# A hybrid recurrent and sparse-attention block on one core: index scores by pairs of heads, recurrence levels over all four quarters of TensorE's array

## What is computed

```python
h = rms_norm(x, norm_mix_pre); z = h @ w_in
# head group 1: RWKV-7, 8 heads of 64, one state (64 x 64) per head, step by step in time
state = state * w_t + (state @ -kk_t) (kk_t * a_t)^T + v_t k_t^T ;  o_t = state @ r_t
# head group 2: sparse attention; an index of 8 heads of 64 chooses the 256 keys of each query
act = relu(einsum('bqhd,bsd->bqsh', qi, ki) * idx_scale)
score = einsum('bqsh,bqh->bqs', act, wi)         # then top-k per query, softmax over those keys
x += rms_norm(concat(y_rwkv, y_attention) @ w_out); x += rms_norm(sqrelu(...) @ w2); x += ...gate...
```

## Time and profile before

| | us |
|---|---|
| median of 3 runs (2139.25 to 2147.84) | 2145.26 |
| profiled execution, and its span | 2152.6, 2150.9 |
| PE busy, PEld busy, DVE busy, ACT busy | 1841.4, 1496.7, 1058.0, 605.5 |
| index scores, first product to last addition | 330.65 to 409.13 |
| recurrence, steps with levels (s = 0 to 7) | 791.5 to 1000 |
| mean granted TensorE clock (share of full speed) | 0.901 |

### The profile page before, as it was taken

The page is one execution under the profiler, slowest core; times in us unless marked ns, Lnnn a source line. Parts: engine busy times, 40 slices in busy tenths (PEclk is TensorE's granted clock), DMA queues, the critical chain, the costliest instruction groups (busy, mean ns, idle before and its releaser), DMA issues. The chain is left out here.

```text
span 2150.9 us, 34217 instructions
## 1 busy us (share of the span) xinstructions
PE 1841.4 (86%) x13992; PEld 1496.7 (70%) x13992; DVE 1058.0 (49%) x1927; ACT 605.5 (28%) x963; POOL 516.4 (24%) x375
## 2 busy tenths in 40 slices
PE   1999968799489969998597699999999999966993
PEld 0876754388367769997486588888888888855782
DVE  6166724599855635775314644253442533536203
ACT  4245413477355533332221200000000000013220
POOL 3133300032022201222243322222222222204233
PEclk9999985699789989998796699999999999985996
DMA  2135440123111050210510011111111111100201
GB/s 99 56 111 174 132 129 27 39 69 115 51 42 40 11 194 28 76 33 15 201 40 20 30 49 48 44 46 46 49 49 49 49 49 49 49 20 0 88 11 78
DMA packets 75000, 134.75 MB, mean 63 GB/s; under 512 B 5824, under 2 KB 49888, under 8 KB 74368
## 3 DMA queue, kind: packets, MB, share of 16 engines
q1 hardware_dynamic: 45760, 118.38, 16.7%
q10 hardware_dynamic: 29120, 14.68, 2.4%
HBM read 96.86 MB, written 36.18 MB: 62 GB/s over the span
## 5 line engine op out<-in xcount | busy, mean ns | idle before, releaser
L440 POOL TENSOR_TENSOR w_ffn_lo<-w_ffn_raw,w_ffn_hi 128x1024 fp32r<-128x1024 f32 x64 | 153.7, 2403 | 547.7 <-ACT w_ffn_hi L436 532.9
L436 ACT ACTIVATE w_ffn_hi<-w_ffn_raw 128x1024 fp32r<-128x1024 f32 x62 | 65.8, 1062 | 614.7 <-PE ffn_acc L463 320.1
L461 PE MATMUL ffn_acc<-h_hi,w_ffn_hi 128*128 128x512 f32 x512 | 200.3, 391 | 10.6 <-DVEq L565 10.6
L462 PE MATMUL ffn_acc<-h_lo,w_ffn_hi 128*128 128x512 f32 x512 | 200.1, 391 | 0.0
L463 PE MATMUL ffn_acc<-h_hi,w_ffn_lo 128*128 128x512 f32 x512 | 200.0, 391 | 0.0
L448 PE MATMUL ffn_acc<-ffn_hi,w_ffn_hi 128*128 128x512 f32 x512 | 199.2, 389 | 0.0
L449 PE MATMUL ffn_acc<-ffn_lo,w_ffn_hi 128*128 128x512 f32 x512 | 199.2, 389 | 0.0
L450 PE MATMUL ffn_acc<-ffn_hi,w_ffn_lo 128*128 128x512 f32 x512 | 199.2, 389 | 0.0
L581 DVE TENSOR_TENSOR y<-y,ffn_acc 128x2048 f32<-128x2048 f32 x32 | 73.2, 2288 | 240.5 <-PE ffn_acc L450 240.5
L461 PE MATMUL z_acc<-h_hi,w_in_first_hi 128*128 128x512 f32 x304 | 122.3, 402 | 14.4 <-ACTq L502 10.4
L573 DVE TENSOR_SCALAR ffn_relu<-ffn_acc 128x1024 f32<-128x1024 f32 x32 | 39.2, 1225 | 169.3 <-PE ffn_acc L463 169.3
(11 more groups left out here) (327 smaller groups left out, 4095.0 us busy)
## 6 DMA issues: line engine op xcount, KB each, us to landing
w_ffn_raw<-w_ffn SPq DMA_DIRECT2D x64, 512.0 KB, 3.5
rwkv_factors<-factors_then_masks ACTq DMA_DIRECT2D x28, 512.0 KB, 6.3
factors<-rwkv_factors SPq DMA_DIRECT2D x32, 448.0 KB, 6.9
w_in_first_raw<-w_in SPq DMA_DIRECT2D x19, 512.0 KB, 4.0
w_in_raw<-w_in SPq DMA_DIRECT2D x12, 512.0 KB, 4.2
x_in<-xT SPq DMA_DIRECT2D x8, 512.0 KB, 6.6
zT<-z_out SPq DMA_DIRECT2D x8, 512.0 KB, 2.9
w_out_raw<-w_out SPq DMA_DIRECT2D x8, 512.0 KB, 4.0
```

The lines of the kernel that those rows point to most:

```text
L436: act.activation(self.hi[u][:, :], self.raw[:, u, :], ACT.Copy).then_inc(self.rounded, 1)
L440: pool.tensor_tensor(self.lo[u][:, :], self.raw[:, u, :], self.hi[u][:, :].bitcast(F32), ALU.subtract).then_inc(self.split, 1)
L461: pe.matmul(acc[:, cut], w.hi[u][:, col], hi[:, k, cut], start=(k == 0), stop=False)
L462: pe.matmul(acc[:, cut], w.hi[u][:, col], lo[:, k, cut], start=False, stop=False)
```

## The change

Index scores: PE takes two heads at a time, one on each half of the array's rows, chunk of keys by chunk of keys, into its own PSUM tensor each; there are two such pairs of tensors and four relu buffers. PE waits for both relus of the pair before the last. The mask is loaded after the first queries.

Recurrence: T and T transposed now lie with chunks in opposite partition halves. The factor A is written with its two chunks exchanged (one DVE instruction becomes two). `levels` does in every slot the `take_x` of one half of the heads together with the `take_sum` of the other, head by head; per head there are then products over all four quarters. It waits for the ACT copy and the DVE merges of both before its first product. `multiply_b` computes one more product per head (8 more per call), since T and its transpose need the product of A and B in both layouts. In `own_chunk` the K·A products go to the opposite column half and another PSUM bank than the K·R products; so ACT waits for `tg_done` before its first copy of piece 4. `copy_x` and `add_level` are now one per slot.

```diff
-                dve.scalar_tensor_tensor(out[:, A_T, :], kk[:, :], -1.0, e_before[:, :], ALU.mult, ALU.mult)
+                for c in range(2):
+                    by_chunk = lambda x: x.rearrange("p (i c t) -> p i c t", i=TILES, c=2)
+                    dve.scalar_tensor_tensor(by_chunk(out[:, A_T, :])[:, :, 1 - c, :], by_chunk(kk[:, :])[:, :, c, :], -1.0, by_chunk(e_before[:, :])[:, :, c, :], ALU.mult, ALU.mult)
...
+    over = ((half[0], half[1]), (half[1], half[0]))
...
-        ps_x = [ctx.pb(f"ps_level_x{h}", [P, HALF], F32) for h in range(2)]
-        ps_t = [ctx.pb(f"ps_level_sum{h}", [P, 2, HH, N], F32) for h in range(2)]
+        ps_l = [ctx.pb(f"ps_level{h}", [P, 4, HH, N], F32) for h in range(2)]
...
+            def levels(hx, hs, sx, ss, lx, ls):
+                x, m = 0 <= sx < TILES, 0 <= ss < TILES
+                if x and lx == 0:
+                    pe.wait_ge(cut1[hx], sx + 1)
+                    pe.wait_ge(t0_ready[hx], sx + 1)
+                elif x:
+                    pe.wait_ge(level_added[hx], LV * sx + lx)
+                if m:
+                    pe.wait_ge(level_x_copied[hs], LV * ss + ls + 1)
+                    need(pe, level_added[hs], LV * ss + ls)
                 for hd in range(HH):
+                    if x:
+                        for a, b in over:
+                            last_x = pe.matmul(ps_l[hx][b, 0, hd, :], mx[hx][sx % 3][a, hd, BA, :], tt[hx][sx % 3][a, 0, hd, :], start=True, stop=True)
+                    if m:
+                        for a, b in over:
+                            last_s = pe.matmul(ps_l[hs][b, 2, hd, :], xs[hs][b, hd, :], tt[hs][ss % 3][b, 1, hd, :], start=True, stop=True)
+                        if ls < LV - 1:
+                            for a, b in over:
+                                last_s = pe.matmul(ps_l[hs][a, 1, hd, :], tt[hs][ss % 3][b, 1, hd, :], xs[hs][b, hd, :], start=True, stop=True)
...
-                    for c in half:
+                    for c, o in over:
                         for e, k in enumerate(half):
-                            pe.matmul(bank[h][c, e, q * 4 * N:(q * 4 + 1) * N], F[k, 2 * h + q, A_T, c], F[k, 2 * h + q, B_T, c], start=True, stop=True)
+                            pe.matmul(bank[h][c, e, q * 4 * N:(q * 4 + 1) * N], F[k, 2 * h + q, A_T, o], F[k, 2 * h + q, B_T, c], start=True, stop=True)
+                            pe.matmul(bank[h][o, e, (q * 4 + 3) * N:(q * 4 + 4) * N], F[k, 2 * h + q, B_T, c], F[k, 2 * h + q, A_T, o], start=True, stop=True)
...
-                    for x, which in enumerate((KA, KR)):
-                        for hd in range(HH):
-                            for c in half:
-                                last = pe.matmul(bank[h][c, 0, (2 * hd + x) * N:(2 * hd + x + 1) * N], mx[h][f % 3][c, hd, which, :],
-                                                 tm[h][f % 3][c, TV, hd % 2, hd // 2, :], start=True, stop=True)
+                    for hd in range(HH):
+                        v = tm[h][f % 3][:, TV, hd % 2, hd // 2, :]
+                        for a, b in over:
+                            pe.matmul(bank[h][b, 0, hd * N:(hd + 1) * N], mx[h][f % 3][a, hd, KA, :], v[a], start=True, stop=True)
+                        for c in half:
+                            last = pe.matmul(bank[h][c, 1, hd * N:(hd + 1) * N], mx[h][f % 3][c, hd, KR, :], v[c], start=True, stop=True)
...
-                for h in range(2):
-                    if n % 2 == 0:
-                        take_x(h, s, n // 2)
-                    else:
-                        take_sum(h, s, n // 2)
+                if n % 2 == 0:
+                    levels(0, 1, s, s if n else s - 1, n // 2, n // 2 - 1 if n else LV - 1)
+                else:
+                    levels(1, 0, s, s, n // 2, n // 2)
...
+                        if 0 <= t < TILES:
+                            act.wait_ge(tg_done[h], t + 1)
                         if f < TILES:
                             act.wait_ge(own_products[h], f + 1)
...
-        rl = ctx.sb("index_relu", [P, 2, SEQ], F32)
-        ps = ctx.pb("ps_index", [P, 2, SEQ], F32)
+        rl = ctx.sb("index_relu", [P, 4, SEQ], F32)
+        ps = [[ctx.pb(f"ps_index{v}{e}", [P, SEQ], F32) for e in range(2)] for v in range(2)]
...
+            for m, (j, t, b) in enumerate(units):
                 keys = (t + 1) * P
                 pe.wait_ge(loaded[j % 2], 16 * (j // 2 + 1))
+                if m >= 2:
+                    pe.wait_ge(relued, 2 * (m - 1))
+                for c in range(0, keys, HALF):
+                    cut = slice(c, min(c + HALF, keys))
+                    for e in range(2):
+                        f = slice(e * IDX, (e + 1) * IDX)
+                        last = pe.matmul(ps[m % 2][e][:, cut], qi[f, j % 2, b, :], kiT[f, cut], start=True, stop=True)
+                last.then_inc(multiplied, 1)

```

More of the change, by code:

```diff
@@ L1209, in own_chunk @@
                     for hd in range(HH):
-                        for c in half:
-                            last = pe.matmul(bank[h][c, 1, hd * N:(hd + 1) * N], tt[h][t % 3][c, 1, hd, :], gg[h][t % 3][c, hd, :], start=True, stop=True)
+                        for a, b in over:
+                            last = pe.matmul(bank[h][a, 0, (HH + hd) * N:(HH + hd + 1) * N], tt[h][t % 3][b, 1, hd, :], gg[h][t % 3][b, hd, :], start=True, stop=True)
                     last.then_inc(tg_done[h], 1)
@@ L1221, in turn_w @@
                     for e, k in enumerate(half):
-                        for j, c in enumerate(half):
-                            last = pe.matmul(bank[h][k, j, q * N:(q + 1) * N], tm[h][t % 3][c, TA, q, e, :], tt[h][t % 3][c, 1, 2 * e + q, :], start=True, stop=True)
+                        for j, (a, b) in enumerate(over):
+                            last = pe.matmul(bank[h][k, j, q * N:(q + 1) * N], tm[h][t % 3][b, TA, q, e, :], tt[h][t % 3][b, 1, 2 * e + q, :], start=True, stop=True)
                 last.then_inc(wt_done[h], 1)
@@ L1367, in _ @@
                 if n % 2:
-                    for h in range(2):
-                        add_level(h, s, n // 2)
+                    add_level(0, s, n // 2)
+                elif n:
+                    add_level(1, s, n // 2 - 1)
+                else:
+                    add_level(1, s - 1, LV - 1)
                 for h, k, at in pieces:
@@ L1520, in _ @@
         @block.scalar
         def _(act):
-            for j, t in enumerate(tiles):
+            for m, (j, t, b) in enumerate(units):
                 keys = (t + 1) * P
-                for h in range(HEADS):
-                    n = j * HEADS + h
-                    act.wait_ge(multiplied, n + 1)
-                    if n >= 2:
-                        act.wait_ge(summed, n - 1)
-                    act.activation(rl[:, n % 2, 0:keys], ps[:, n % 2, 0:keys], ACT.Relu, scale=IDX ** -0.5).then_inc(relued, 1)
+                act.wait_ge(multiplied, m + 1)
+                for e in range(2):
+                    n = 2 * m + e
+                    if n >= 4:
+                        act.wait_ge(summed, n - 3)
+                    act.activation(rl[:, n % 4, 0:keys], ps[m % 2][e][:, 0:keys], ACT.Relu, scale=IDX ** -0.5).then_inc(relued, 1)
```

85 lines of the change are left out of this document (30 added, 55 removed).

## The result

| | us |
|---|---|
| before, median (beside the changed kernel) | 2146.55 |
| after, median (lowest to highest of four) | 2119.58 (2117.07 to 2122.38) |
| ratio, 95% interval | 0.9879 (0.985 to 0.9908) |
| forecast | 2100 (2080 to 2130) |
| after, profiled execution | 2117.07, span 2115.2 |

The change saves about 26 us, 1.2%. I had forecast 45.6: 27 in the index scores and 18.6 in the recurrence. The first came, the second did not.

The account below looks back on a forecast made before the run. It took latencies between PE and ACT to bound the index scores and PE the recurrence. Savings of 27 + 18.6 = 45.6 us from 2152.6 gave 2107.0, less 7.3 for the median 2099.7, forecast as 2100, range 2080 to 2130.

Parts of the forecast that it names:

- Index scores: Index scores: the wait for relu n - 2 goes, DVE bounds, the clock rises early; end at 381, 27 us saved.
- rival 2: Index scores: the clock stays at 0.50 and PE is the bound, 17.4 us saved there; 2109 us, chance 0.12.
- rival 5: Index scores: the gain fails as ACT and DVE pace each other, only the recurrence counts; 2127 us, chance 0.03.
- The units: Recurrence levels: a unit of four heads on four quarters takes 0.95 us instead of 1.38, -4.3 us a step.
- my two bounds: `multiply_b` in the recurrence: 1.35 us at the same 28 ns, 1.15 at the four-quarter pace; 1.3 taken.
- rival 3: Recurrence: same-row neighbours do not overlap, unit 1.38 us, steps of 29.0 us; 2130 us, chance 0.12.
- Waits between engines: Recurrence: PE waits in slots 3, 6, 7, 8 and at slot 0, with a few small ones 1.9 us a step.
- rival 1: Recurrence: no waits, DVE's free third is used fully, the whole 36 us gained; 2082 us, chance 0.13.
- rival 4: Recurrence: DVE is late in every slot, the 0.93 us chain stands bare ten times a step; 2156 us, chance 0.05.
- The step that failed: Recurrence: PE is busy for 162.9 of 164.0 us in six steps, so PE work saved counts there.
- My own sign of being wrong: Wrong if units take 1.3 us, steps are under 23.5 or over 26.5 us, or the index clock stays at 0.50.
- the forecast step of 24.7 us: Recurrence: 22.8 us of PE work plus 1.9 us of waits, 24.7 us a step instead of 27.3.

Follow-up runs that it names:

- e5_after_wide_levels: Changed kernel with each two level products of 64 columns made one of 128 (some values wrong): 2098.4 us, ratio 0.9768.
- the first stream: Kernel before with 1024 products of 64x64 on all four quarters, without waits, put ahead of the recurrence: 4096 instructions in 56.2 us.
- e12_stream_long_loops: Kernel before with three-turn loops of 64x64 four-quarter products ahead of the recurrence: turns of 1792, 2016 and 2304 instructions took 52.2, 86.5 and 111 us.

## Why the prediction was right and where it was wrong

**Index scores: right, by the mechanism and the size.** End 380.8 for 381, DVE the bound, the clock at 1.00 from 335 on; 27.5 us alone for 27. Rivals 2 and 5 are out.

**The units: right.** The windows view of one unit and of one `multiply_b` after:

```profile
759.29:760.21 0.92, 0.92 (x47) 0.92 (x48) 0.00 (x0) 0.82 (x1) 0.00 (x0) 1.00 1.01 401
...
864.26:865.30 1.04, 1.04 (x65) 1.04 (x62) 0.97 (x9) 0.38 (x1) 0.00 (x0) 1.00 0.00 0
```

A unit takes 0.92 us (forecast 0.95), the own chunk's 32 records 0.50 (0.48). `multiply_b` takes 1.04 where I took 1.3: its off-diagonal records fill free quarters, so the four-quarter end of my two bounds (1.15) was the nearer one. Same-row neighbours overlap and share a bank, as the rows had said; rival 3 is out.

**Waits between engines: right in place, too large in size.** 0.9 us a step where I had 1.9, at L1260 and L1133. Waits for packets can hide some of them: with fewer instructions, in `e5_after_wide_levels`, the same two rows are 6.3 us, 1.3 a step. Rivals 1 and 4 are out.

**The step that failed** is the sentence "PE never waits, so work saved on PE counts there, until another engine or a latency is late". There was a third case, PE's own instruction supply, and I had no rival for it. My own sign of being wrong, steps of over 26.5 us, was met: they take 27.4. By my terms the five steps should have taken 5 x 24.7 = 123.5 us. The stalls called issue rose by 21.8 - 6.3 = 15.5, the waits for VectorE were 5 x 1.9 - 4.6 = 4.9 less than costed: 134.1. The 3.1 us left to 137.2 are not split further; they are rather 7, since the units and `multiply_b` came out some 0.7 us a step below what I had costed. Two parts of them are known in kind only: the clock at 0.94 in one step, the one with the longest stall (1.9 us), and my start from 27.3 us a step, where these five took 27.6 before. An estimate from the stream says how much was to be had at most: 36 packets at 3.5 us are 126 us, 25.2 a step, if every packet came at its earliest. By this estimate the forecast step of 24.7 us was just out of reach with these instructions, even without any wait.

I could have seen it. The page of the kernel before lists the queue, and its DMA view gives 34 packets for the same five steps, one in 4.1 us. PE's records came at 63 per us (1728 in the 27.3 us of the last row of before), and my new unit asks for 104. The change also adds 64 records a step (8 extra products in each of two calls of `multiply_b`, four records each), which costs the scarce thing to save the plentiful one: the 17 us of array time that the change saved brought nothing, while each instruction costs 14 ns in a stream that is bound by its packets (3.6 us / 256).

**The sum.** 27 came and 18.6 did not. The measured 2119.6 lies in the range, but none of my cases describes it: 2130 (rival 3) and 2127 (rival 5) stood near it for reasons that the runs exclude, and the range held it only because it reached to them. That the number lies inside is luck as far as the recurrence goes.

## What to carry to other kernels

Count instructions, not only array time: take the packets of the instruction queue in a stage, multiply by the closest distance that any stretch shows (3.4 to 3.6 us here), and treat the result as one more engine. A fp32 product of 64x64 is four instructions, and they run in 30 ns on four quarters and 60 on two, where the supply allows 56; small products, written out, reached that limit here on four quarters and not on two; wider products, or a loop whose body the engine still holds, move it away. An idle time called "issue" in the middle of a group that has no wait in the program is its sign.

## What the runs showed of the hardware that I had not expected

- A stream without waits stalls 1.4 to 1.6 us in every 256 instructions; four quarters with 64 columns are only 9% faster than two in the long run (56.2 and 61.5 us for 1024 products), though a burst runs at 15 ns a pass against 29.
- The engine reads ahead by a few packets at most: the first stream ran 758 records, three packets' worth, before it stalled for the first time. Yet what was fetched is kept: a loop of 1792 instructions ran its second and third turn without a packet, one of 2016 did not. The Trainium skill, "Runtime: NRT & Kernel Launch", Instruction fetch mechanics, gives the tensor engine room for 2048 instructions. The loop of 1792 agrees with that; one of 2016 would fit by the number alone and was fetched again. The same section says that kernels prefer full unrolling where possible; in this case that cost 10 us of 28 (a stream written out against 16 turns of 128).
- Beside loads of 9.2 MB (243 GB/s over the stream) the distance of the packets doubled at worst, to 7.3 us.
- Two products of 64x64 that share their rows but not their columns run side by side at 15 ns a pass, with weights loaded for each (1792 passes in 26.43 us in `e12_stream_long_loops`).
